# The first block's gate and mixing projections by seven products of quarters

## The reference

```python
u = rms_norm(x, norm_g) * (1 + scale[:, None]) + shift[:, None]
z = u @ w_in
(aq, ak, av, ag, iq, ik, iw, bq, bk, bv, bg, cq, ck, cv, cg, ma, mb, mc) = jnp.split(z, SPLIT_OFFSETS, axis=-1)
# ya, yb, yc: sparse (top-k), windowed and stick-breaking attention, 512 wide each
ya = ya * silu(ag); yb = yb * silu(bg); yc = yc * silu(cg)
merged = (sigmoid(ma) * (ya @ w_br_a) + sigmoid(mb) * (yb @ w_br_b) + sigmoid(mc) * (yc @ w_br_c))
return x + gate[:, None] * (merged @ w_out)
```

## Time and profile before

| | us |
|---|---|
| median of 3 runs | 1471.54 (1470.56 to 1472.87) |
| the profiled execution | 1472.5 |
| its span, first to last instruction | 1470.8 |
| PE busy | 1412.7 (96%) |
| PEld busy | 1153.9 (78%) |
| DVE busy | 563.2 (38%) |
| ACT busy | 414.6 (28%) |
| POOL busy | 156.8 (11%) |
| L872, 3200 matmul records of 256 columns | 718.3 busy |
| mean granted TensorE clock | 0.994 of 2.4 GHz |

### The profile page before, as it was taken

How to read it: one execution, slowest core, us unless ns; L and a number is a source line. 1 busy time by engine, 2 the same in 40 slices (tenths; PEclk the granted TensorE clock), 3 DMA queues, 4 the chain that set the end, 5 groups by cost and what they waited for, 6 DMA issues and landing times.

```text
span 1470.8 us, 20226 instructions
## 1 busy us (share of the span) xinstructions
PE 1412.7 (96%) x8130; PEld 1153.9 (78%) x8130; DVE 563.2 (38%) x1335; ACT 414.6 (28%) x771; POOL 156.8 (11%) x191
## 2 busy tenths in 40 slices
PE   5999999999999999999999999999989999999996
PEld 3888788888878888888888888877767788877765
DVE  1363312211226432313235431245663532466453
ACT  1112212412011222333323312331333422433432
POOL 0110200000011030000111100003230000133100
PEclk9999999999999999999999999999999999999999
DMA  8644544355445444443333332455323433332200
GB/s 356 240 153 171 206 166 166 131 196 197 182 172 215 180 172 172 146 182 117 142 122 136 115 126 104 143 200 201 115 69 148 156 136 110 141 115 86 87 29 29
DMA packets 31485, 221.76 MB, mean 151 GB/s; under 512 B 3872, under 2 KB 4000, under 8 KB 4896
## 3 DMA queue, kind: packets, MB, share of 16 engines
q1 hardware_dynamic: 31392, 220.47, 40.5%
HBM read 219.41 MB, written 1.05 MB: 150 GB/s over the span
## 4 chain that ended last, share of the span: by engine, by line
PE 84%; DVE 7%; ACT 2%; issue 2%; POOL 2%; DMA 1%; DVEq 0%; SPq 0%; ACTq 0%; POOLq 0%
PE event L872 43%; PE event L863 9%; PE event L1016 6%; PE event L1060 5%; PE logits L948 3%; PE mixed_out L1004 3%; PE event L829 3%; PE event L1028 2%; PE turns L967 2%; PE event L1160 1%; DMA ring<-in_w 1%; PE event L1087 1%; PE event L1041 1%; DVE logits L1605 1%; PE event L851 1%
## 5 line engine op out<-in xcount | busy, mean ns | idle before, releaser
L872 PE MATMUL event<-u,ring 128*128 128x256 f32 x3200 | 718.3, 383 | 14.2 <-ACT u L1371 6.1
L872 PEld LDWEIGHTS event<-u,ring 128*128 128x128 f32 x3200 | 604.8, 191 | 113.4 <-issue 30.1
L863 PE MATMUL event<-ring,u 128*128 128x256 f32 (+1 forms) x704 | 150.9, 371 | 0.0
L863 PEld LDWEIGHTS event<-ring,u 128*128 128x128 f32 x704 | 127.4, 190 | 20.9 <-issue 4.9
L1968 POOL TENSOR_TENSOR raw<-raw,tables 128x512 f32<-128x512 f32 (+1 forms) x28 | 44.7, 1595 | 763.3 <-DVE turned L1581 455.4
L1241 ACT ACTIVATE region<-event 128x512 f32<-128x512 f32 x72 | 43.0, 597 | 279.9 <-PE event L872 279.7
L1277 ACT ACTIVATE S<-logits,stat 128x512 f32<-128x512 f32 (+2 forms) x160 | 83.7, 534 | 127.9 <-DVE stat L1620 123.2
L1060 PE MATMUL event<-region,ring 128*128 128x256 f32 x384 | 85.2, 380 | 2.9 <-DVE region L1763 2.9
L1016 PE MATMUL event<-region,ring 128*128 128x256 f32 x384 | 84.4, 380 | 0.0
L1060 PEld LDWEIGHTS event<-region,ring 128*128 128x128 f32 x384 | 72.2, 190 | 15.2 <-issue 5.9
L1016 PEld LDWEIGHTS event<-region,ring 128*128 128x128 f32 x384 | 72.6, 190 | 11.1 <-issue 1.4
(11 more groups left out here) (208 smaller groups left out, 1270.7 us busy)
## 6 DMA issues: line engine op xcount, KB each, us to landing
ring<-in_w SPq DMA_DIRECT2D x204, 1024.0 KB, 4.8
tables<-in_two SPq DMA_DIRECT2D x1, 1472.0 KB, 7.8
x<-in_x SPq DMA_DIRECT2D x1, 1024.0 KB, 17.4
x<-in_ctx SPq DMA_DIRECT2D x1, 1024.0 KB, 6.5
out<-x SPq DMA_DIRECT2D x4, 256.0 KB, 2.2
tables<-in_one SPq DMA_DIRECT2D x1, 768.0 KB, 8.2
tables<-in_late SPq DMA_DIRECT2D x1, 512.0 KB, 5.6
consts<-in_common SPq DMA_DIRECT2D x1, 320.0 KB, 3.3
```

The lines of the kernel that those rows point to most:

```text
L863: ins = mm(bank[:, t * 256:t * 256 + width], mem.u[:, q, k, t * P:(t + 1) * P], wt[:, k * 256:k * 256 + width], start=k == 0, stop=k == KB ...
L872: ins = mm(bank[:, j * 256:(j + 1) * 256], wt[:, k * 256 + j * P:k * 256 + j * P + P], mem.u[:, q, k, :], start=k == 0, stop=k == KB - 1)
```

## The change

**Seven products.** For the gate and mixing units the weights W (1024 x 256) and the input u (1024 x 256 tokens) are cut into quarters: by depth (blocks 0 to 3 and 4 to 7), by output channels (128 and 128) and by tokens (128 and 128). The four quarters of the result, eight products of quarters before, are made of seven (Winograd's form of Strassen's scheme). The item is ("fast", name, i, (0,)), takes the place of ("proj", ...) and uses two events, a left bank with three products (the first two for the upper left quarter of the result, the third from sums on both sides) and a right bank with four. TensorE does it in two halves by depth (h), each 6 matmuls into the left and 8 into the right bank, 128 x 128 x 128 each.

**Sums of weights**, for each unit and half: GpSimd forms S3 = A11 - A21, A21 := A21 + A22 in the ring slot, and S2 = A21 - A11; VectorE forms S4 = A12 - S2. Three sets of places (`wsum`) serve the halves in turn: GpSimd waits for the half three before to be spent. `with_sums` puts ("sum", n, 0) and ("sum", n, 1) ahead of the unit that stands before the n-th fast unit, on both engines' lists.

**Sums of inputs**, once in a section: ("tsum", 0) and ("tsum", 1) on VectorE, around the last av unit; they use `raw`, `turned` and the quarter of `u` that no later unit of the section reads.

**Merging.** ScalarE copies the first product out of the left bank, VectorE adds in four operations, and both banks are free. ("gates",) and ("sig", i) now wait for VectorE's drains. The mixing columns keep room for two thirds at a time (4096 instead of 6144 elements), the rest is for the sums.

**Banks dealt on.** A section's first event takes the bank after the last one of the section before (`phase`).

**One input sooner.** In two0, ("feed", 1, "v1") stands between the two halves of the latent `hi` unit, ahead of ("logits", 7), and no longer behind that unit.

```diff
+def with_sums(s):
+    units = [n for n, i in enumerate(s) if i[0] in ("proj", "merge", "out", "fast")]
+    first = {}
+    count = 0
+    for a, b in zip(units, units[1:]):
+        if s[b][0] == "fast":
+            first[a] = [("sum", count, 0), ("sum", count, 1)]
+            count += 1
...
-            [proj("ak", 0, 1), ("rot", "ak", 0)], [proj("av"), ("rot", "ak", 1)], [proj("av", 0, 1)]]
+            [proj("ak", 0, 1), ("rot", "ak", 0)], [proj("av"), ("rot", "ak", 1)], [("tsum", 0), proj("av", 0, 1), ("tsum", 1)]]
...
-    fill += [[proj("gate", 0, i)] for i in range(6)] + [[proj("m", 0, i)] for i in range(4)]
+    fill += [[fast("gate", i)] for i in range(6)] + [[fast("m", i)] for i in range(4)]
...
-                      proj("fq"), ("rot", "fk", 0), ("mod", "v1"), proj("fv"), ("rot", "fq", 0), proj("hi"), ("feed", 1, "v1"), proj("ff", 1),
+                      proj("fq"), ("rot", "fk", 0), ("mod", "v1"), proj("fv"), ("rot", "fq", 0), ("half", proj("hi")), ("feed", 1, "v1"), proj("hi"), proj("ff", 1),
...
+        self.phase = (before.phase + before.total) % BANKS if before else 0
...
-        e = u = 0
+        e, u = self.sec.phase, 0
...
# tensor
+            elif kind == "fast":
+                n = sec.index(item)
+                if n == 0:
+                    eng.wait_ge(sems["t_ready"], w.at("t_ready", 1))
+                left, right = mem.bank[e % BANKS], mem.bank[(e + 1) % BANKS]
+                ts = mem.tsum
+                for h in range(2):
+                    eng.wait_ge(sems["summed"], w.at("summed", 2 * n + h + 1))
+                    s2, s3, s4 = mem.wsum[(2 * n + h) % 3]
+                    for bank in (left, right):
+                        if h == 0:
+                            ev = e if bank is left else e + 1
+                            eng.wait_ge(drained[ev % BANKS], w.fills(ev - BANKS))
+                        order = (0, 1, 2) if bank is left else (0, 2, 1, 3)
+                        for p in order:
+                            for i in range(2):
...
+                                if bank is left:
+                                    lhs, rhs = ((wt[:, low:low + P], b11), (wt[:, high:high + P], b21), (s2[:, i, :], ts[2][:, k, :]))[p]
+                                else:
+                                    lhs, rhs = ((s3[:, i, :], ts[3][:, k, :]), (wt[:, high + P:high + 256], ts[4][:, k, :]),
+                                                (wt[:, low + P:low + 256], ts[1][:, k, :]), (s4[:, i, :], b22))[p]
+                                ins = mm(bank[:, p * P:(p + 1) * P], lhs, rhs, ...)
+                        if h == 1:
+                            ins.then_inc(full[(e if bank is left else e + 1) % BANKS], 1)
+                    if h == 0:
+                        ins.then_inc(sems["spent"], 1)
...
# vector
+            elif kind == "sum":
...
+                eng.wait_ge(sems["partial"], w.at("partial", 2 * n + h + 1))
+                tt(s4, a12, s2, ALU.subtract).then_inc(sems["summed"], 1)
...
+            elif kind == "fast":
...
+                eng.wait_ge(sems["first_copied"], w.at("first_copied", sec.index(item) + 1))
+                tt(upper, left[:, 1:3, :], lower[:, 0:1, :].broadcast_to([P, 2, P]), ALU.add).then_inc(drained[e % BANKS], 1)
+                eng.wait_ge(drained[e % BANKS], w.fills(e))
+                eng.wait_ge(full[(e + 1) % BANKS], w.fills(e + 1))
+                tt(both, right[:, 0:3:2, :], upper[:, 1:2, :].broadcast_to([P, 2, P]), ALU.add).then_inc(mine, 1)
+                eng.wait_ge(mine, w.linked())
+                tt(lower, right[:, 1:3, :], both[:, 0:1, :].broadcast_to([P, 2, P]), ALU.add)
+                tt(upper[:, 1, :], right[:, 3, :], both[:, 1, :], ALU.add).then_inc(drained[(e + 1) % BANKS], 1)
...
# pool
+            elif kind == "sum":
...
+                if g >= 3 and g % 2 == 1:
+                    eng.wait_ge(sems["spent"], w.at("spent", (g - 3) // 2 + 1))
+                elif g >= 3:
+                    ev = sec.event(sec.fasts()[(g - 3) // 2]) + 1
+                    eng.wait_ge(full[ev % BANKS], w.fills(ev))
+                tt(s3, a11, a21, ALU.subtract).then_inc(mine, 1)
+                eng.wait_ge(mine, w.linked())
+                tt(a21, a21, a22, ALU.add).then_inc(mine, 1)
+                eng.wait_ge(mine, w.linked())
+                tt(s2, a21, a11, ALU.subtract).then_inc(sems["partial"], 1)
```

More of the change, by code:

```diff
@@ L93, in softmaxes @@
     return sum(j.kind != "C" for j in jobs[:n])
-UNIT_KINDS = ("mva", "proj", "merge", "out", "outa", "outb")
+UNIT_KINDS = ("mva", "proj", "merge", "out", "outa", "outb", "fast")
 EARLY, LATE = (0, 1, 2, 3, 6, 7), (4, 5)
@@ L169, in proj, with fast @@
     return ("proj", name, i, (q,))
+def fast(name, i):
+    return ("fast", name, i, (0,))
+def with_sums(s):
[6 more added lines that the diff above has]
+            count += 1
+    out = []
+    for n, item in enumerate(s):
+        out += first.get(n, []) + [item]
+    return out
 def one_start():
@@ L263, in lay @@
             pieces[-1] += item
+        elif item[0] == "half":
+            pieces.append([item])
+        elif has_unit(item) and [("half", item)] == (pieces or [[]])[-1][:1]:
+            pieces.append([item])
         elif has_unit(item):
@@ L343, in __init__ @@
         n = {}
-        events = sum(self.events(i) for i in script)
+        self.total = sum(self.events(i) for i in script)
+        self.phase = (before.phase + before.total) % BANKS if before else 0
         for b in range(BANKS):
-            n[f"full{b}"] = n[f"drained{b}"] = len(range(b, events, BANKS))
+            n[f"full{b}"] = n[f"drained{b}"] = sum(e % BANKS == b for e in range(self.phase, self.phase + self.total))
         for q in ("logits_ready", "exps_done", "probs_ready", "turned", "turns_copied", "mixed", "y_copied"):
@@ L349, in __init__ @@
         n["maxed"] = softmaxes(jobs, len(jobs))
+        n["summed"] = n["partial"] = 2 * kinds.count("fast")
+        n["spent"] = n["first_copied"] = kinds.count("fast")
+        n["t_ready"] = sum(i == ("tsum", 1) for i in script)
         n["rope_done"] = n["shuffled"] = n["sine_done"] = kinds.count("rot")
@@ L378, in events @@
             return item[1] % 2
[L379 removed]
+        return {"proj": 1, "out": 1, "ada": 1, "stats": 1, "outa": 1, "outb": 4, "merge": 2, "fast": 2, "norm": 1, "level": 2, "khatT": 2, "state": 1,
                 "hout": 1, "mean": 1, "var": 1}.get(kind, 0)
@@ L578, in __init__ @@
         self.merged = blocks(region[:, 0:2048])
+        left = [r["sums"][:, i * 256:(i + 1) * 256] for i in range(8)] + [self.turned[:, 1, 0:256]]
+        self.wsum = [[a.rearrange("p (k n) -> p k n", n=P) for a in left[3 * i:3 * i + 3]] for i in range(3)]
+        T1 = self.u[:, 0, 0:4, P:T]
+        T2, T3, T4 = (a.rearrange("p (k n) -> p k n", n=P) for a in (self.raw[:, 0, :], self.raw[:, 1, :], self.turned[:, 0, :]))
+        self.tsum = {1: T1, 2: T2, 3: T3, 4: T4}
         t = self.tables
@@ L1244, in body @@
                     exps()
+            elif kind == "fast":
+                name, i = item[1], item[2] if item[1] == "gate" else item[2] % 8
+                eng.wait_ge(full[e % BANKS], w.fills(e))
+                act(mem.one[name][:, 2 * i + 1, 0:P], mem.bank[e % BANKS][:, 0:P], ACT.Copy).then_inc(sems["first_copied"], 1)
+                eng.wait_ge(sems["first_copied"], w.at("first_copied", sec.index(item) + 1))
             elif kind == "silu":
@@ L1295, in body @@
             elif kind == "gates":
+                for ev in latest(*(w.first[fast("gate", i)] + 1 for i in range(6))):
+                    eng.wait_ge(drained[ev % BANKS], w.fills(ev))
                 g = mem.one["gate"][:, :, :]
@@ L1300, in body @@
             elif kind == "sig":
-                m = mem.one["m"][:, KB * item[1]:KB * (item[1] + 1), :]
+                for ev in latest(*(w.first[fast("m", 4 * item[1] + i)] + 1 for i in range(4))):
+                    eng.wait_ge(drained[ev % BANKS], w.fills(ev))
+                m = mem.one["m"][:, KB * (item[1] % 2):KB * (item[1] % 2) + KB, :]
                 act(m, m, ACT.Sigmoid).then_inc(sems["sig_done"], 1)
@@ L1754, in body @@
                     eng.wait_ge(full[(e + n) % BANKS], w.fills(e + n))
-                    src, gate, out = split2(mem.bank[(e + n) % BANKS]), mem.one["m"][:, KB * br + b:KB * br + b + 2, :], \
+                    src, gate, out = split2(mem.bank[(e + n) % BANKS]), mem.one["m"][:, KB * (br % 2) + b:KB * (br % 2) + b + 2, :], \
                         mem.merged[:, b:b + 2, :]
```

102 lines of the change are left out of this document (77 added, 25 removed).

## The result

The changed kernel takes 1487.7 us (median of 4 runs, 1485.5 to 1489.1); the kernel before takes 1471.1 (4 runs, 1469.1 to 1472.9). The ratio is 1.0113, 95% interval 1.0101 to 1.0125: **slower by 16.7 us**, where 12.4 faster was predicted.

The account below looks back on a forecast made before the run. TensorE, busy 96% of the span, was taken as the bound. Quarters 3.1 us (26.6 - 21.9 waits - 1.6 clock), input 5.3 and banks 4.0 sum to 12.4 less: 1459 us from a median of 1471.54; 8-in-10 range 1441 to 1469.

Parts of the forecast that it names:

- Seven products for eight: Gate and mixing units on TensorE: 6.2 us a unit for 6.94, 36 units, 26.6 us less work, bounds 23 to 30.
- rival D: Weight loads bound the narrow matmuls, a unit taking 10.6 us: 1617 us; chance 0.01.
- (a): First unit of the first section: TensorE waits 2.2 us for sums behind GpSimd's masking, between 0.8 and 3.
- (b): Behind the job with the eight longest maxima and exponentials: late masking, sums and conditioning copy cost 6.3 us, bounds 2 and 9.
- (c): First section, behind the gates: left bank waits for ScalarE's late copy and VectorE's gating delays the next sum, 2.2 us.
- (d): Second section, around the sixth unit: masking delay meets a normalisation needing a third bank, 4.8 us, bounds 1 and 6.
- (e): Second section, behind the gates: sums stand behind VectorE's gating and the forget-gate scans, 4.9 us, bounds 2 and 8.
- (f): Eight later units among level and merge steps with VectorE nearly free: an allowance of 1.5 us, 0 to 5.
- The clock: After longer TensorE waits the clock falls to 1.2 GHz and slows following records: 1.6 us added for one case.
- One input sooner: Context's modulated input formed ahead of the maxima: TensorE starts at about 1085.8, gain 5.3 us, between 0 and 7.7.
- B: Rival: VectorE and GpSimd hold each other up in runs of units, 1483 us, 1471 if half happens; chance 0.10.
- A: Rival: the waits are mostly absorbed, only some 9 us remain, 1444 us (1438 to 1450); chance 0.26.

Follow-up runs that it names:

- Experiment 8: Changed kernel with matmuls on stale data filling five TensorE waits, half as many as in a first try: 1481.7 us, ratio 1.0077.
- experiment 2: Kernel before with only the block's input formed sooner in the second block's first section: 1473.8 us, ratio 1.0028.
- experiment 1: Kernel before with only the banks dealt on across the sections: 1468.4 us, ratio 0.9985.
- Experiment 14: 12 with the scan's first two VectorE steps put one unit later each: 1446.7 us, ratio 0.9847 to the kernel before.
- experiment 5: Changed kernel with the fourth sum of weights moved from VectorE to GpSimd, so all four are there: 1466.2 us, ratio 0.9964 to the kernel before.
- experiment 9: Changed kernel with all four sums on GpSimd and the block's input back at its old place: 1462.5 us, ratio 0.9940 to the kernel before.
- 12: experiment 11 with VectorE's three products of branch and gate each behind another unit: 1457.4 us, ratio 0.9898 to the kernel before.
- experiment 11: experiment 9 with each fast unit's first product copied by VectorE in place of ScalarE: 1454.6 us, ratio 0.9888 to the kernel before.

## Why the prediction was wrong, by its steps

**Seven products for eight: right in kind, 3.8 us too large.** 6.25 us a unit for 6.2 in a long run, but 6.37 against 7.00 between other work, so 22.8 us for 26.6, just under the lower bound of 23. The term priced both units by their steady rate. The load rule of rival D has no part: 56 loads stand beside the 56 records of a unit. (The Trainium skill, TensorE: Matmul & The Clock Gate, Part 3, would have had them one after the other; this trace does not agree.)

**The waits: the places right, most sizes too small.** Predicted and measured: (a) first unit 2.2 and 4.68; (b) eight-map job 6.3 and 3.9 (1.01 + 2.40 + 0.53; the conditioning part of 2.0 did not come); (c) 2.2 and 2.11; (d) 4.8 and 6.7 (5.14 + 1.58); (e) 4.9 and 5.5; (f) 1.5 and 3.9; with two small ones, 0.9 in the gate stretch, 27.8 us for 21.9. Two durations were behind it. I priced GpSimd's step at 0.70; in a row of steps it came every 0.80 (0.72 to 0.79 and a hand-over). And VectorE's sum at 0.42; where a step of GpSimd had just begun it took 0.98, so that a pair of half units took 5.9 us from GpSimd's first step to the last sum (242.09 to 247.97), and not 4.2 + 0.45. In (a) the same shows in four places: GpSimd's masking ended 0.7 nearer to TensorE's logits than in the kernel before, its six steps took 5.1 us for 4.2, the sum 0.98 for 0.42, and the last token quarter 1.17 for 0.69. (f) was an allowance, not a walk, and the poorest term.

**The clock, the term of this sum that was mis-sized most.** I added 1.6 us once. There were four cases, 10.1 us. I had the waits of 4.8 and 3.4 us in my own list and the row of 2.33 us that already slowed 32 records by 1.7, and yet counted "two or three" and priced one. Experiment 8 shows that the slowing belongs to the idle time. Together: 22.8 - 27.8 - 10.1 = 15.1 us slower where I had 3.1 faster. The stages say 17.5 slower. Of the other 2.4, 1.0 is the second section's first block (64 records in 15.78 us, before 14.76), which is as slow in experiment 2 too, whose first two sections are those of the kernel before, so it is no effect of the sums; 1.4 I could not place.

**One input sooner: wrong in sign.** Predicted 5.3 gained; lost 4.1 alone by the ratio and 6.2 in place by the medians, 2.1 and 3.3 in the traces. Between the profile with the banks alone and that of the changed kernel it is 2.0 (304.0 and 306.0). The step that failed: "VectorE is free for it at 1084.56, so TensorE starts at about 1085.8". I followed the input's own chain and gave back 2.4 us at the *next* level step. I did not ask what else the waiting matmul needs: its bank, copied by ScalarE behind the very softmax that the input now overtakes.

**Banks dealt on: right,** 4.1 us of stage for 4.0, though 1.7 of it is slow records that the wait does not bring every time (experiment 1).

**The whole.** 17.5 slower in the stages with new units, 2.1 faster in the third (4.1 - 2.0), 0.4 faster in the rest, 1.6 slower ahead of the logits: 16.6 us, the difference of the two spans. The steps that failed are thus the price of a wait (one slow stretch of 1.6 us where four cost 10.1), the waits themselves (21.9 for 27.8), the chain of the input moved ahead, and the steady rate taken for a unit (3.8).

**Rivals.** B had the right side and 1483 for 1487.7, but by another way: steady runs of units do keep up, and GpSimd's steps stayed at means of 0.756 to 0.776, with single ones up to 1.6. Its sense was right in part, since 19 of VectorE's 72 sums took over 0.85 us and their mean was 0.60 where I had 0.42. (The Trainium skill, SBUF — State Buffer, "Who interferes with whom", names such pairs; the trace agrees for these, and shows the size.) A, all absorbed, is excluded. Experiment 14 lies near its figure (1446.7; A said 1444), partly by luck: A counted 5.3 us for the input, which 14 has at its old place, and no saving of order that 14 makes. Still it shows what the seven products can bring once the lists are in the right order. My chances were too sure: that the lists are strict I held against A, and not against my own durations, of which every one that runs long lengthens a wait.

## What to carry to other kernels

When an engine gets help from two others in a chain, count the chain's places in each list and not its busy time: VectorE at 45% cost 21.5 us, mainly because it stood waiting ahead of work that was ready. Give a chain of small steps to one engine, even the slower one, and expect that each cause removed uncovers the next in another list (sums, then ScalarE's copy, then the scan): go on until the trace names none. To a wait of TensorE belong the slow records behind it (in the changed kernel's profile 1.9 to 3.2 us to each wait of 2.4 to 5.1), and before moving an input ahead, list *all* that its consumer waits for.

## What the runs showed of the hardware

- **GpSimd and VectorE beside each other, both on SBUF.** VectorE's 256-element sum: 0.42 us alone, 0.98 where GpSimd's step had begun just before (244.51 behind 244.49). Where VectorE began first (252.35), its sum took 0.42 and GpSimd's step 0.95. VectorE's merges, with one input in a bank, kept to 0.42 to 0.43 beside GpSimd. GpSimd's step: 0.72 to 0.79, but 1.6 beside VectorE's gating of 1024 elements, which itself took 1.57 a piece instead of 1.25 (4.71 us for three, 3.74):

```profile
702.76 4.71 DVE L1815 TENSOR_TENSOR region<-region 128x1024 f32<-128x1024 f32 x3 [5.80 <-ACT region L1380]
...
704.80 1.58 POOL L2125 TENSOR_TENSOR ring<-ring 128x256 f32<-128x256 f32 x1
706.47 1.58 POOL L2127 TENSOR_TENSOR region<-ring 128x256 f32<-128x256 f32 x1
```

- **The clock after idle time.** In the changed kernel it stayed at 1.00 behind the wait of 2.11 us at 295.04 and was 0.50, the 1.2 GHz level, behind 2.40, 4.68, 4.74 and 5.14; in experiment 5 it stayed behind 0.77 and 1.17. Between these the length alone does not decide: behind the wait of 1.83 us at 281.18 in experiment 5 it fell and at 279.33 in experiment 9 it did not, behind 1.94 us in 12 it fell and in 14 it did not, and behind the 2.33 us at the border it fell in the kernel before and not in experiment 2. In experiment 11 it fell behind a wait of 1.93 us, but only 1 us after TensorE had started again, at 771.30. Stretches of that trace (PEclk is the number behind the five busy times):

```profile
771.30:772.30 1.00, 1.00 (x9) 1.00 (x10) 0.97 (x3) 0.31 (x1) 0.92 (x2) 1.00 0.71 295
772.30:774.00 1.70, 1.70 (x12) 1.70 (x11) 0.06 (x1) 0.74 (x1) 1.54 (x3) 0.58 0.00 0
774.00:776.00 2.00, 2.00 (x11) 2.00 (x11) 0.00 (x0) 0.00 (x0) 1.76 (x4) 0.50 0.00 0
```

  So the first record behind a wait does not tell whether the wait will be paid twice, and one profile does not tell it for the next execution.
- **The first 180 us vary.** In the sixteen profiles the same logits start at 175.1 to 181.1 us. In the two profiles of the kernels before and changed the difference of 1.6 us is the granted clock around 40 us; in the others the cause stays open. A difference of 2 us between two single profiles is none.
